# Value products that take their PSUM banks one token tile at a time, and a compressed score and a compressed turn that move in between them

## The reference, cut to what matters

```python
proj = rms_norm(h, ln1_w) @ w_in
(q, kc, vc, ks, vs, kw, vw, gate, rq, rk, rv, rg) = jnp.split(proj, ...)
# compressed attention: 31 keys, each made of 32 tokens
s_cmp = jnp.einsum('bgrqd,bgcd->bgrqc', q, k_cmp) * scale
p_cmp = masked_softmax(s_cmp, cmask)
o_cmp = jnp.einsum('bgrqc,bgcd->bgrqd', p_cmp, v_cmp)
# retention
inner = jnp.einsum('bhqd,bhkd->bhqk', rope(rq), rope(rk) * dk ** -0.5) * dmat
y = jnp.einsum('bhqk,bhkv->bhqv', inner, rv) + ...
```

## Time and profile before

| what | value |
|---|---|
| median of 3 runs | 1462.97 us (1460.94 to 1463.64) |
| the profiled execution, its own time | 1461.55 us |
| its span | 1459.8 us |
| PE busy | 1424.6 us, 98% of the span |
| POOL, DVE, ACT busy | 678.4, 857.8, 583.8 us |
| HBM read, written | 169.79 MB, 12.59 MB |

### The profile page before, as it was taken

One profiled execution on the slowest core, in us unless ns is written; L12 is line 12 of the kernel. 1 busy time (PEld: TensorE's weight loads), 2 busy tenths in 40 slices (PEclk: granted clock), 3 DMA queues, 4 the chain that ended last, 5 costly groups with the idle time before them and its releaser, 6 DMA issues.

```text
span 1459.8 us, 19175 instructions
## 1 busy us (share of the span) xinstructions
PE 1424.6 (98%) x7138; PEld 1155.2 (79%) x7138; DVE 857.8 (59%) x1419; ACT 583.8 (40%) x786; POOL 678.4 (46%) x516
## 2 busy tenths in 40 slices
PE   7999999999999999999999999999989999999997
PEld 6776866788888888887888878888867888888886
DVE  4457467549767788976772565356675333332357
ACT  4476467352221221225344665543353322332231
POOL 4433345426556465553452334355524544544553
PEclk9999999999999999999999999999989999999999
DMA  8421300235656464233955433354322232232222
GB/s 316 145 115 60 144 1 2 73 112 180 238 169 235 158 215 145 88 114 101 126 182 142 155 126 127 122 209 148 112 97 91 87 116 87 87 110 92 87 89 84
DMA packets 50837, 185.79 MB, mean 127 GB/s; under 512 B 15104, under 2 KB 16512, under 8 KB 36032
## 3 DMA queue, kind: packets, MB, share of 16 engines
q1 hardware_dynamic: 43264, 170.99, 34.4%
q10 hardware_dynamic: 7488, 13.63, 3.1%
HBM read 169.79 MB, written 12.59 MB: 125 GB/s over the span
## 4 chain that ended last, share of the span: by engine, by line
PE 80%; DVE 3%; ACT 1%; issue 0%; POOL 0%; DVEq 0%; ACTq 0%
PE bank L453 16%; PE bank L455 16%; PE bank L454 16%; PE bank L512 8%; PE bank L514 8%; PE bank L513 8%; PE bank L480 1%; PE bank L929 1%; PE bank L801 1%; PE bank L958 1%; DVE Alo L1718 1%; PE bank L703 1%; PE bank L902 1%; PE bank L895 0%; DVE X L2483 0%
## 5 line engine op out<-in xcount | busy, mean ns | idle before, releaser
L1573 POOL TENSOR_TENSOR wlo<-raw,whi 128x512 fp32r<-128x512 f32 x424 | 609.6, 1469 | 648.4 <-ACT whi L1041 648.4
L453 PE MATMUL bank<-Ahi,whi 128*128 128x512 f32 x1024 | 405.7, 396 | 3.4 <-DVE Alo L1718 2.7
L455 PE MATMUL bank<-Ahi,wlo 128*128 128x512 f32 x1024 | 399.5, 390 | 0.0
L454 PE MATMUL bank<-Alo,whi 128*128 128x512 f32 x1024 | 399.4, 390 | 0.0
L1041 ACT ACTIVATE whi<-raw 128x2048 fp32r<-128x2048 f32 x111 | 212.7, 1916 | 229.5 <-PE bank L514 193.9
L453 PEld LDWEIGHTS bank<-Ahi,whi 128*128 128x128 f32 x1024 | 192.8, 188 | 49.0 <-issue 4.7
L455 PEld LDWEIGHTS bank<-Ahi,wlo 128*128 128x128 f32 x1024 | 192.6, 188 | 40.7
L454 PEld LDWEIGHTS bank<-Alo,whi 128*128 128x128 f32 x1024 | 192.8, 188 | 39.3 <-issue 0.7
L512 PE MATMUL bank<-whi,Bhi 128*128 128x512 f32 x496 | 193.2, 389 | 1.1 <-DVEq L1952 1.1
L514 PE MATMUL bank<-whi,Blo 128*128 128x512 f32 x496 | 193.0, 389 | 0.0
L513 PE MATMUL bank<-wlo,Bhi 128*128 128x512 f32 x496 | 193.0, 389 | 0.0
(11 more groups left out here) (406 smaller groups left out, 1940.3 us busy)
## 6 DMA issues: line engine op xcount, KB each, us to landing
raw<-in_ws SPq DMA_DIRECT2D x112, 1024.0 KB, 5.0
adaw<-in_ada SPq DMA_DIRECT2D x48, 512.0 KB, 4.6
spill<-stage ACTq DMA_DIRECT2D x32, 256.0 KB, 2.1
X<-in_x SPq DMA_DIRECT2D x8, 512.0 KB, 6.9
gates<-spill SPq DMA_DIRECT2D x16, 256.0 KB, 5.3
w1k<-in_w1k SPq DMA_DIRECT2D x1, 2048.0 KB, 15.8
w1v<-in_w1v SPq DMA_DIRECT2D x1, 2048.0 KB, 9.5
XM<-spill ACTq DMA_DIRECT2D x8, 256.0 KB, 3.0
```

What stands on the lines that cost most here:

```text
L453: pe.matmul(ps[:], wh, hi[:, k], start=(k == 0), stop=False)
L454: pe.matmul(ps[:], wh, lo[:, k], start=False, stop=False)
L455: ins = pe.matmul(ps[:], wl, hi[:, k], start=False, stop=(k == kn - 1))
L1573: pool.tensor_tensor(wlo[slot][:, part], raw[slot][:, part], rd(whi[slot][:, part]), ALU.subtract).then_inc(sem("lo_split"), 1)
```

## The change

It does three things. First, `value_runs` takes a bank for token tile i only when part 0 of that tile begins, and in the order O, O, G, G, so that tiles 0 and 1 go to pool O. Second, on the PE `compressed_turn(0)` moves from ahead of the product of rk1 (c = 11) to behind it, `compressed_scores(3)` moves in behind (0,0) of `rv`, `compressed_turn(1)` in behind (0,1), and the first retention scores from behind (0,1) to behind (0,2). Third, on ACT `c_turned(0)` moves behind rk1's copy, and `c_exp(3)` and `c_turned(1)` behind the rounding of the second weight tile of `rv`. DVE's, POOL's and SP's orders stay.

```diff
-                outs = [bank("G"), bank("G"), bank("O"), bank("O")]
+                outs = []
 
                 def run(q, i):
+                    if q == 0:
+                        outs.append(bank("OOGG"[i]))
                     ks = split[q]
...
                     if q:
                         done(ins, f"{name}t{i}", outs[i][1])
+                        product[f"{name}.1"] = outs[i][1]
...
-                product[f"{name}.1"] = outs[NT - 1][1]
...
                 if c == 11:
-                    compressed_scores(3)
-                if c >= 10:
-                    compressed_turn(c - 10)
+                    compressed_turn(0)
             run = value_runs("rv")
             for x, (q, i) in enumerate(STAGGERED):
                 run(q, i)
-                if x == 1:
+                if x == 0:
+                    compressed_scores(3)
+                elif x == 1:
+                    compressed_turn(1)
+                elif x == 2:
                     retention_scores(0, (0, 1))
                 elif x == 3:
                     retention_scores(0, (2, 3))
...
                     hi_upto(last_tile(INDEX["rv.1"]))
+                    c_exp(3)
+                    c_turned(1)
                     halves_turned(WIN[c - 1])
...
-                if 8 <= c < 12:
+                if 8 <= c < 11:
                     c_exp(c - 8)
-                if 10 <= c < 12:
-                    c_turned(c - 10)
+                if c == 11:
+                    c_turned(0)
```

## The result

| | before | changed |
|---|---|---|
| median of 20 runs | 1462.08 us (1459.82 to 1463.64) | 1464.55 us (1463.17 to 1465.71) |
| span of the profiled execution | 1459.8 us | 1462.3 us |
| granted PE clock, mean over the span | 0.993 | 0.991 |

The ratio is 1.0019, 95% interval 1.0013 to 1.0026: the changed kernel is 2.5 us slower by the medians. The forecast was +2.75 us, on top of the median of three runs, which lay 0.9 us above this median of 20. The busy times are those of before to 1 us; what differs is the time that the PE idles and its clock.

A forecast was written before the change was run, and what follows sets the result against it. The prediction took the PE to bound the kernel, busy 1424.6 of 1459.8 us. Its terms, -0.45 + 1.5 + 1.7 = +2.75 us on the median 1462.97, gave 1465.7 us, range 1460.0 to 1468.0.

The forecast's parts named there:

- First term: At va: PE starts 1.2 us earlier, but kc's rope, tile 4's load and q0's copy only 0.45 earlier; -0.45 us.
- Second term: At rv: later exponential and meeting POOL delay DVE's RW, so second retention scores wait and (0,3) starts later; +1.5 us.
- Third term: Behind the new PE wait at rv the clock falls to 1.2 GHz, on the path ahead of (0,3); +1.7 us.
- The sum: Whole kernel: -0.45 + 1.5 + 1.7 = +2.75 us, profiled execution 1464.3 us, 1465.7 on the median.
- The longer fall: Rival at rv: 1.2 GHz begins earlier and lasts through (0,3) and (1,1), costing 3.4; +4.45 us, 1467.4; chance 0.20.
- The wait without the fall: Rival at rv: PE waits for DVE but the clock does not fall; +1.05 us, 1464.0; chance 0.14.
- the closed gaps: Rival: DVE's chain does not hold the second retention scores, gaps simply close; -3.2 to -4.9 us, middle 1459.0; chance 0.12.
- the change that hides itself: Rival at rv: DVE and POOL meet less, RW as before or up to 1.6 earlier; -2.0 to +1.2 us; chance 0.12.

The follow-up runs named there:

- f8: Kernel of e1 with SP's load of weight tile 4 moved ahead of the small loads of kc and vc; 1455.9 us, ratio 0.9962 to the kernel before.
- g1: Changed kernel with va asking for its four banks at once again, rv kept the new way; a single execution, 1463.92 us.
- f6: Second run of e2's kernel, the changed kernel with 16 unused matmuls filling the PE's wait; 1463.31 us, ratio 1.0013 to the kernel before.
- e2: Changed kernel plus 16 matmuls of unused product in the PE's wait at the second retention scores; 1463.22 us, ratio 1.0017 to the kernel before.
- e1: Changed kernel with DVE doing four RW products ahead of rope of rq1, four ahead of rope of rk1; 1457.2 us, ratio 0.9974 to before.
- e3: Changed kernel with ACT's exponential of query tile 3 and ct1's copy moved ahead of rounding weight tile 9; 1465.07 us, ratio 1.0026 to before.
- e4: Kernel before with only the bank part of the change (taken tile by tile, idle ones first), no step moved; 1460.25 us, ratio 0.9995.
- f5: Changed kernel run once more as it is, beside f6 on one chip; 1464.69 us, ratio 1.0023 to the kernel before.
- f7: Kernel before with e1's DVE order alone; 1461.24 us, ratio 1.0000 to the kernel before.

## Why the prediction was right

**First term, -0.45.** The direction and the place hold (f8): the PE had 1.2 us at `va` and lost most of it at the squares of q0 (0.94 of wait), because tile 4's load stood behind kc's rope. The size is not confirmed. The squares of q0 came 0.27 us earlier against the span's start, 0.07 against the last matmul of kc and vc, and g1, without the change at `va`, had them no later than the changed kernel. Two details of the step were off. I had L1757, the middle rope instruction, wait for POOL's last quarter; it got through, and the last one waited:

```profile
37.12 1.66 DVE L1760 TENSOR_TENSOR K<-K,F 128x512 f32<-128x512 f32 x1
```

with the same end, 38.78 for my 38.8, and SP's small loads began at 38.86 instead of 39.34, the 0.45 almost exactly. But these loads then went through faster by 0.7 us, so SP issued tile 4's load 1.16 us earlier (46.10 for 47.26), and the load itself took 0.9 us longer: ACT began to round it at 51.85, only 0.26 before. Neither was in my sum.

**Second term, +1.5.** The step that carries the forecast, and the one that the runs confirm best: in the filled kernels, where the clock doesn't fall, (0,3) lies 1.53 (f6) and 1.48 us (e2) later against the squares of q1 than before. The exponential ended at 127.63 for 127.9, DVE idled 1.39 for 1.37, `RW` came 1.55 us later against the squares of q1 for 1.5, the PE waited 4.0 for 3.5. (0,3) started at 140.47 for 140.4, of which 0.3 belong to the clock. e1 takes the late banks away, with the exponential as late as ever, and wins 3.7 us against before; e3 takes the late exponential away and wins back only 0.4 us of the 1.55. e4, with two of the three gaps closed and the exponential left where it was, wins nothing. So the cost goes through DVE's fixed order, as the step has it, and in it the late exponential and POOL's earlier quarters stand in for each other: to take the first away alone leaves 1.16 of the 1.55 us.

**Third term, +1.7.** The fall of the clock behind the new wait is there and its cause is shown (e2, f6). In the traces it is larger than I had it: 2.9 us in the first (2.6 of it from (0,3) to the first retention value product, 16.88 against 14.27), 2.0 in the second. In the timed runs filling the wait gave back 1.4 us beside the changed kernel. So the size was right within what can be told from the times, and too small for both traces. That the earlier fall, behind the old gap, cost nothing on the path, as I had it, e4 bears out: it is gone there, and (0,3) lies where it lay.

**The sum** met the profiled execution partly by luck. At the first retention value product the changed kernel was 4.2 us behind (157.35 for 153.18), more than my 2.75; 1.7 us of it came back near 192 us, where the trace of before has a stretch at 1.2 GHz and this one hasn't, which leaves the 2.5 us between the spans. The timed runs gave 2.5 us and, in f5, 3.8; their intervals overlap, and both hold the forecast.

**The rivals.** The longer fall happened in the first trace: 10.24 us at 1.2 GHz, 4.6 of them ahead of (0,3), where the PE mostly waited, so that they cost 2.9 us and not the 3.4 that I had priced. The wait without the fall is out, since every trace with the wait and no fill has the fall. So are the closed gaps, (0,3) being 1.56 us later instead of some 3 earlier, and the change that hides itself, `RW` being 1.55 us later.

## What to carry to other kernels

Before a wait on the busiest engine is removed, follow what comes next in time on each of the other engines, not only the wait itself: here the gaps that were closed led up to another engine's chain that was just in time. A step that is moved behind a long one on ACT takes with it all that waits for it in DVE's fixed order, and what frees a bank should stand ahead of what nobody waits for yet: that order gained more here (e1) than moving the step back (e3). And a change that loses 2.5 us alone and one that measures nothing alone can be worth 3.7 us together.

## What the runs showed of the hardware

- DVE products of 128x512 with both inputs in SBUF take 0.69 us alone and 1.33 to 1.76 where they meet POOL's quarters; POOL's quarter takes 1.25 alone (5.00 for four in f7) and up to 1.7 (6.70 for four before). The `RW` products, which read one input from PSUM, take 0.74 or less beside POOL (2.94 for four, e1 and f7). Moving DVE work earlier into POOL's stretch gave 0.4 of 1.39 us (e3).
- The clock fell behind waits that were not long one by one: 1.20 and 1.70 us before, and 0.57, 0.72, 0.72, 1.97 and 0.70 us in e3, each with some matmuls between them.
- The stretch at 1.2 GHz near 190 us is in some traces of one and the same kernel and not in others, with the same wait of 1.61 us ahead of it (before, changed, f5, f6); 3.4 us of it are worth 1.7 us, as much as a whole term of this prediction.
- From its issue to ACT's rounding, the 1 MB load behind the same ten small ones took 4.85 us before, 4.97 in g1, 5.21 in e1 and 5.75 in the changed kernel; why is open.
